# Second mixer: the forget term of the scores as a two-row product, the chunk mask as two more rows of queries and keys

## The reference, cut to what matters

```python
key_unit = jnp.arange(s) // causal_unit            # causal_unit: 64 in branch b, 1 in branch c
sc = jnp.einsum('bqhd,bkhd->bhqk', q_blk, k) * scale
if f_blk is not None:                              # branch c: F[t] - F[s]
    sc = sc + f_blk.transpose(0, 2, 1)[..., None] - f_k
mask = key_unit[None, :] <= q_unit[:, None]
sc = jnp.where(mask[None, None], sc, -jnp.inf)
p = jax.nn.softmax(sc, axis=-1)
...
log_f = jax.nn.log_sigmoid(c_f + b_forget)
f_cum = jnp.cumsum(log_f, axis=1)
out_c = block_causal_attention(heads(c_q), heads(c_k), heads(c_v), 1, f_cum)
```

## Time and profile before

| | |
|---|---|
| median of three runs | 2592.27 us (2592.19 to 2593.72) |
| profiled execution, its own time | 2591.27 us |
| its span, first to last instruction | 2589.5 us |
| TensorE busy | 2457.9 us, 95% of the span |
| VectorE busy | 1532.7 us, 59% |
| ScalarE busy | 1380.5 us, 53% |
| GpSimd busy | 185.5 us, 7% |
| mean granted clock of TensorE | 0.98 |

### The profile page before, as it was taken

How to read it: one execution, slowest core, us unless ns; L and a number is a source line. 1 busy time by engine, 2 the same in 40 slices (tenths; PEclk the granted TensorE clock), 3 DMA queues, 4 the chain that set the end, 5 groups by cost and what they waited for, 6 DMA issues and landing times.

```text
span 2589.5 us, 42657 instructions
## 1 busy us (share of the span) xinstructions
PE 2457.9 (95%) x17457; PEld 2289.9 (88%) x17457; DVE 1532.7 (59%) x1826; ACT 1380.5 (53%) x1828; POOL 185.5 (7%) x197
## 2 busy tenths in 40 slices
PE   7999999998999999999999999999889999997998
PEld 7998988998998998998999899898879988896997
DVE  5555667645555555567755555576575556747554
ACT  5555777255555545678535554545644444564443
POOL 0000113000000000012300000000030001003000
PEclk9999999999999999999999999999999999998999
DMA  6554443134554554443215456443345554334453
GB/s 220 185 180 146 147 131 115 66 122 150 178 184 162 178 183 159 147 144 126 90 54 175 148 192 206 146 129 109 120 130 183 190 182 141 120 113 148 154 184 125
DMA packets 312111, 385.89 MB, mean 149 GB/s; under 512 B 10780, under 2 KB 287280, under 8 KB 311984
## 3 DMA queue, kind: packets, MB, share of 16 engines
q1 hardware_dynamic: 311704, 384.00, 45.2%
q10 hardware_dynamic: 280, 0.10, 0.0%
HBM read 383.02 MB, written 1.06 MB: 148 GB/s over the span
## 4 chain that ended last, share of the span: by engine, by line
PE 75%; DVE 10%; ACT 9%; issue 4%; DMA 0%; POOL 0%; SPq 0%; DVEq 0%; ACTq 0%; POOLq 0%
PE bank L266 22%; PE bank L267 21%; PE bank L268 21%; DVE wlo L258 4%; ACT whi L252 4%; DVE arena L966 1%; PE bank L1237 1%; PE bank L1232 1%; PE bank L352 1%; PE bank L725 1%; DVE arena L2011 1%; ACT arena L1910 1%; ACT arena L318 1%; PE bank L1243 1%; PE bank L1209 1%
## 5 line engine op out<-in xcount | busy, mean ns | idle before, releaser
L258 DVE TENSOR_TENSOR wlo<-raw,whi 128x2048 fp32r<-128x2048 f32 x360 | 831.9, 2312 | 497.3 <-ACT whi L252 496.3
L266 PE MATMUL bank<-xhi,whi 128*128 128x256 f32 x3712 | 1065.5, 287 | 11.6 <-DVE arena L553 6.8
L267 PE MATMUL bank<-xlo,whi 128*128 128x256 f32 x3712 | 1053.5, 284 | 0.0
L268 PE MATMUL bank<-xhi,wlo 128*128 128x256 f32 x3712 | 1053.2, 284 | 0.0
L252 ACT ACTIVATE whi<-raw 128x2048 fp32r<-128x2048 f32 x360 | 681.7, 1903 | 104.7 <-PE bank L268 101.5
L266 PEld LDWEIGHTS bank<-xhi,whi 128*128 128x128 f32 x3712 | 715.0, 193 | 22.6 <-issue 16.8
L267 PEld LDWEIGHTS bank<-xlo,whi 128*128 128x128 f32 x3712 | 715.3, 193 | 4.9 <-issue 1.9
L268 PEld LDWEIGHTS bank<-xhi,wlo 128*128 128x128 f32 x3712 | 715.0, 193 | 0.0
L266 PE MATMUL bank<-whi,yhi 128*128 128x512 f32 x608 | 238.0, 391 | 9.2 <-ACT yhi L475 6.2
L267 PE MATMUL bank<-wlo,yhi 128*128 128x512 f32 x608 | 237.4, 390 | 0.0
L268 PE MATMUL bank<-whi,ylo 128*128 128x512 f32 x608 | 236.6, 389 | 0.0
(11 more groups left out here) (377 smaller groups left out, 2863.6 us busy)
## 6 DMA issues: line engine op xcount, KB each, us to landing
raw<-in_w_in SPq DMA_DIRECT2D x92, 1024.0 KB, 5.0
raw<-in_ffn_w_in SPq DMA_DIRECT2D x88, 1024.0 KB, 5.0
raw<-in_ffn_w_out SPq DMA_DIRECT2D x44, 1024.0 KB, 4.8
raw<-in_w_gate SPq DMA_DIRECT2D x32, 1024.0 KB, 5.4
raw<-in_w_up SPq DMA_DIRECT2D x32, 1024.0 KB, 5.5
raw<-in_w_down SPq DMA_DIRECT2D x32, 1024.0 KB, 4.8
raw<-in_w_branch_b SPq DMA_DIRECT2D x8, 1024.0 KB, 4.8
raw<-in_w_branch_a SPq DMA_DIRECT2D x8, 1024.0 KB, 4.8
```

The source lines that it names most:

```text
L258: e.tensor_tensor(wlo[s][:], raw[s][:], whi[s][:].bitcast(F32), ALU.subtract).then_inc(lo_done[s], 1)
L266: e.matmul(o, ahi, bhi, start=start, stop=False, skip_group_check=True)
L267: e.matmul(o, ahi, blo, start=False, stop=False, skip_group_check=True)
L268: return e.matmul(o, alo, bhi, start=False, stop=stop, skip_group_check=True)
```

## The change

Branch b: the queries get two more partitions (96 and 97) with the mask's value in one chunk of 64 and zero in the other, the keys two with ones and zeros, so that the score product over 98 partitions adds the chunk mask itself. VectorE writes these rows once per layer, at n = 8. Branch c: GpSimd spreads the log forget values, with sign plus and minus, into two columns of 32 for each head (`forget`); TensorE makes their running sums once, at n = 9, with three products into bank 4; VectorE takes them at n = 10 into `cum_q` and `cum_k`, whose two partitions 32h and 32h + 1 hold for head h the sum and ones, crosswise; and a head's forget term is one product over these two partitions in place of two (first 128 queries) and four (the rest). The tables `minus` and `chunk` leave the constants, two columns `even` and `odd` come in.

```diff
         def scores_b(e, h, o):
-            e.matmul(o[:, 0:128], bqh[0:96, h, 0:P], bkh[0:96, h, 0:P], start=True, stop=False, skip_group_check=True)
-            e.matmul(o[:, 0:128], mask_chunk, ident, start=False, stop=True, skip_group_check=True)
-            e.matmul(o[:, 128:384], bqh[0:96, h, P:T], bkh[0:96, h, :], start=True, stop=False, skip_group_check=True)
-            return e.matmul(o[:, 256:384], mask_chunk, ident, start=False, stop=True, skip_group_check=True)
+            e.matmul(o[:, 0:128], bqh[0:98, h, 0:P], bkh[0:98, h, 0:P], start=True, stop=True, skip_group_check=True)
+            return e.matmul(o[:, 128:384], bqh[0:98, h, P:T], bkh[0:98, h, :], start=True, stop=True, skip_group_check=True)
 
         def scores_c(e, h, o):
             p = slice(HD * (h % 2), HD * (h % 2) + HD)
             b = h // 2
-            G = CG[h % 2]
+            two = slice(32 * h, 32 * h + 2)
             k = dict(skip_group_check=True)
             e.matmul(o[:, 0:128], cq[p, b, 0:P], ck[p, b, 0:P], start=True, stop=False, **k)
-            e.matmul(o[:, 0:128], G[:, 0:128], ones2[:, 0:P], start=False, stop=False, **k)
-            e.matmul(o[:, 0:128], minus, G[:, 0:128], start=False, stop=False, **k)
+            e.matmul(o[:, 0:128], cum_q[two, 0:P], cum_k[two, 0:P], start=False, stop=False, **k)
             e.matmul(o[:, 0:128], mask_causal, ident, start=False, stop=True, **k)
             e.matmul(o[:, 128:384], cq[p, b, P:T], ck[p, b, :], start=True, stop=False, **k)
-            e.matmul(o[:, 128:384], G[:, 128:256], ones2, start=False, stop=False, **k)
-            e.matmul(o[:, 128:384], G[:, 256:384], ones2, start=False, stop=False, **k)
-            e.matmul(o[:, 128:384], minus, G[:, 0:256], start=False, stop=False, **k)
-            e.matmul(o[:, 256:384], minus, G[:, 256:384], start=False, stop=False, **k)
+            e.matmul(o[:, 128:384], cum_q[two, P:T], cum_k[two, :], start=False, stop=False, **k)
             return e.matmul(o[:, 256:384], mask_causal, ident, start=False, stop=True, **k)
+
+        def sums_pe(e, l):
+
+            e.wait_ge(*W["forget"](l))
+            e.wait_ge(*W["rope_done"](l, 1))
+            e.matmul(bank[4][:, 0:P], forget[:, 0, :], le, start=True, stop=True)
+            e.matmul(bank[4][:, P:T], forget[:, 0, :], ones, start=True, stop=False)
+            e.matmul(bank[4][:, P:T], forget[:, 1, :], le, start=False, stop=True).then_inc(W["sums"].sem, 1)
+
+        def mask_rows_dve(e, l):
+            for head, first, second in ((bqh, 0, MASKED), (bkh, 1, 1.0)):
+                rows = head[96:98, :, :].rearrange("p h (b i n) -> p h b i n", b=2, i=2)
+                e.memset(rows[:, :, :, 1 - first, :], 0.0)
+                for b, which in enumerate((even, odd)):
+                    up = e.tensor_scalar(rows[:, :, b, first, :], ones2[96:98, 0:64].unsqueeze(1).to_broadcast([2, H2, 64]),
+                                         which[96:98, :], second, ALU.mult, ALU.mult)
+            up.then_inc(W["mask_rows"].sem, 1)
+
+        def sums_dve(e, l):
+            e.wait_ge(*W["sums"](l))
+            e.tensor_scalar(cum_q, bank[4][:, 0:T], even, odd, ALU.mult, ALU.add)
+            e.tensor_scalar(cum_k, bank[4][:, 0:T], odd, even, ALU.mult, ALU.add).then_inc(W["sums_kept"].sem, 1)
@@ -1688,6 +1705,8 @@
                     values_pe(e, l, head2(n, 3))
+                if n == 9:
+                    sums_pe(e, l)
                 if n == MEAN_AT:
@@ -1756,9 +1775,10 @@
                 e.wait_ge(*W["rope_done"](l, 2))
+                e.wait_ge(*W["mask_rows"](l))
             else:
                 e.wait_ge(*W["kept"](l, 8))
-                e.wait_ge(*W["cg"](l, h))
+                e.wait_ge(*W["sums_kept"](l))
@@ -2019,6 +2039,10 @@
                     rope_dve(e, l)
+                if n == 8:
+                    mask_rows_dve(e, l)
+                if n == 10:
+                    sums_dve(e, l)
@@ -2096,19 +2120,20 @@
+            e.wait_ge(*W["lat_n"](l))
+            finish_waits(e)
+            e.memset(forget, 0.0).then_inc(W["forget_zero"].sem, 1)
             e.wait_ge(*W["lf"](l))
-            for h in range(H2):
-                if h >= 2:
-                    e.wait_ge(*W["scores"](l, 8 + h - 2))
-                finish_waits(e)
-                for a, (m, c) in enumerate(((le, 0), (ones, 0), (le, 1))):
-                    up = e.tensor_scalar(CG[h % 2][:, a * P:(a + 1) * P], m, lf[:, c * H2 + h:c * H2 + h + 1], None,
-                                         ALU.mult)
-                up.then_inc(W["cg"].sem, 1)
+            e.wait_ge(*W["forget_zero"](l))
+            finish_waits(e)
+            for i, sign in enumerate((1.0, -1.0)):
+                up = e.tensor_scalar(forget.rearrange("p c (h n) -> p c h n", n=32)[:, :, :, i],
+                                     lf.rearrange("p (c h) -> p c h", c=TT), sign, None, ALU.mult)
+            up.then_inc(W["forget"].sem, 1)
```

More of the change, by code:

```diff
@@ L93, in constants_2 @@
     freq[64:96, 0] = np.tile(inv_freq, 2)
-    parts = {"ones2": np.ones((P, T)), "minus": -np.ones((P, P)),
-             "chunk": np.where(r // 64 > c // 64, MASKED, 0.0), "causal": np.where(r > c, MASKED, 0.0),
-             "turn": turn, "freq": freq, "flip": r + c == P - 1}
+    parts = {"ones2": np.ones((P, T)), "causal": np.where(r > c, MASKED, 0.0),
+             "turn": turn, "freq": freq, "flip": r + c == P - 1,
+             "even": i[:, None] % 32 == 0, "odd": i[:, None] % 32 == 1}
     at, where = 0, {}
@@ L1517, in hybrid_stack_kernel @@
         rtmp = blk(17472)
-        CG = [blk(17984 + i * 384, 384) for i in range(2)]
+        forget = blk(17984, 256).rearrange("p (c n) -> p c n", c=TT)
+        cum_q, cum_k = blk(18240, 256), blk(18496, 256)
         table2 = blk(18944, CONSTANTS2.shape[1])
@@ L1532, in const2 @@
             return table2[:, a:b]
-        ones2, minus, mask_chunk, mask_causal, turn, freq, flip = [const2(n) for n in ("ones2", "minus", "chunk", "causal",
-                                                                                       "turn", "freq", "flip")]
+        ones2, mask_causal, turn, freq, flip, even, odd = [const2(n) for n in ("ones2", "causal", "turn", "freq", "flip",
+                                                                               "even", "odd")]
         cf_raw, cf_hi, cf_lo = [w[:, :, 0:H2] for w in ba_w]
@@ L1547, in hybrid_stack_kernel @@
             lf_shift=1, rowmax=12, bias_masked=1,
-            cg=4, scores=12, maxed=12, expd=12, inv=12, scaled=12, p_turned=12, pt_kept=12, o_product=12, o_hi=6, o_lo=6,
+            forget_zero=1, forget=1, sums=1, sums_kept=1, mask_rows=1, scores=12, maxed=12, expd=12, inv=12, scaled=12, p_turned=12, pt_kept=12, o_product=12, o_hi=6, o_lo=6,
             tap=31, mean=1, centred=1, c_sq=1, c_var=1, c_ln=1, c_r=1, c_norm=1, c_bias=1, c_abs=1, c_exp=1, c_l=1,
@@ L2098, in mix2_pool @@
             e.wait_ge(*W["bias_masked"](l))
+            e.wait_ge(*W["lat_n"](l))
+            finish_waits(e)
+            e.memset(forget, 0.0).then_inc(W["forget_zero"].sem, 1)
             e.wait_ge(*W["lf"](l))
-            for h in range(H2):
-                if h >= 2:
-                    e.wait_ge(*W["scores"](l, 8 + h - 2))
-                finish_waits(e)
-                for a, (m, c) in enumerate(((le, 0), (ones, 0), (le, 1))):
-                    up = e.tensor_scalar(CG[h % 2][:, a * P:(a + 1) * P], m, lf[:, c * H2 + h:c * H2 + h + 1], None,
-                                         ALU.mult)
-                up.then_inc(W["cg"].sem, 1)
[L2108 to L2111, removed]
+            e.wait_ge(*W["forget_zero"](l))
[4 more added lines that the diff above has]
+            up.then_inc(W["forget"].sem, 1)
+            e.wait_ge(*W["d_sig"](l))
+            finish_waits(e)
+            u = dpad[:, :, CONV_K - 1:]
+            e.tensor_tensor(u, u, rtmp2.rearrange("p (c t) -> p c t", c=2), ALU.mult).then_inc(W["u_done"].sem, 1)
             e.wait_ge(*W["c_sig"](l))
```

## The result

The changed kernel takes 2598.81 us (median of 17 runs, 2596.12 to 2602.94) against 2591.76 us before (17 runs, 2589.82 to 2595.4): ratio 1.0027, interval 1.0019 to 1.0034, so slower by 7 us. The profiled execution took 2596.32 us, 2.5 us under the median; its mean granted clock is 0.977, where the three slowest of the 17 (2600.93 to 2602.94 us) have 0.975 and the kernel before has 0.980, so its trace shows somewhat less lost clock than a slow execution has.

A forecast was written before the change was run, and what follows sets the result against it. TensorE was taken as the bound, joined to a VectorE-ScalarE ring. Per stage +2.24 + 0.66 - 0.44 - 4.40 = -1.94, twice -3.88, with one clock fall +1.68: -2.2, so 2590.1 us on the median; range 2585.0 to 2597.0.

The forecast's parts named there:

- Mask rows: Six VectorE instructions at n = 8 that nothing hides: 2.24 us per stage; TensorE then stands 2.63 us.
- the dearer of its two rows: For a memset of 512 elements, the two-input operation's step of about 0.60 us, taken over the copy's about 0.35.
- The clock: Granted clock falls to 0.50 behind TensorE's stall at n = 9, in one stage of two, costing 1.68 us.
- Branch c's head: Each head of branch c takes 2.74 us instead of 3.84, gaining 1.10 per head and 4.40 per stage.
- a dear return and a cheap fall: In branch c's heads, returning to 128 contracted rows costs 0.30 us, falling to fewer rows 0.10.
- Sums and branch b: Sums on TensorE at n = 9 add 0.66 us per stage; branch b's shorter scores gain 0.44.
- The ring: VectorE-ScalarE loop not limiting branch c; rival has it bind at n = 16 to 19: 2591.7 us, chance 0.12.
- The two-row rival: Changes of rows around branch c's two-row products eat all 1.10 us per head: +6.6 us, 2598.9, chance 0.10.

The follow-up runs named there:

- e1: Kernel before plus only the six mask-row instructions on VectorE at n = 8, unread: 2602.63 us, ratio 1.0036.
- e2: Kernel before with branch b's part alone, mask rows at n = 8, branch c as before: 2602.58 us, ratio 1.0038.
- e4: Whole change with the mask rows moved from n = 8 to n = 5: 2590.08 us, ratio 0.9994.
- e9: Kernel before with branch b's part alone, mask rows at n = 5: 2594.77 us, ratio 1.0010.
- e3: Kernel before with branch c's part alone, no mask rows, branch b keeping its mask products: 2587.19 us, ratio 0.9979.
- e6: e4 with a branch c head's products grouped 64, 64, 2, 2, 128, 128 rows; output lacks a part: 2587.79 us, ratio 0.9983.
- e11: Kernel before with branch c's part alone, products grouped by rows, sums at n = 13 and 14: 2582.39 us, ratio 0.9962.
- e8: e7 with the grouped product order of e6, including its missing output part: 2581.20 us, ratio 0.9954.
- e10: e8 with start=False in the second product, so that everything is computed: 2583.27 us, ratio 0.9968.
- e5: e4 with the forget product contracting 64 partitions in place of two, which changes the output: 2588.42 us, ratio 0.9987.
- e7: e4 with the sums moved to n = 13 on TensorE and n = 14 on VectorE: 2595.01 us, ratio 1.0008.

## Why the prediction was wrong

The forecast was 2590.1 us, -2.2; the median went up 7.0, past the range's end. In the profiled execution the spans differ by +5.1, 7.3 more than forecast, and the terms tell where:

- **Mask rows.** Right in kind and nearly in size: 2.36 us where 2.24 was forecast, and the stall 2.75 where 2.63 was. Twice 0.12 is 0.2 us. The tensor_scalars step 0.26 us as read; what is left of the 2.36, 1.32 us, are the two memsets, 0.66 each with the short idle time in front, where 0.60 was taken. The Trainium skill, VectorE: DVE Perf Modes, section Zero memsets can be issued as uint32 (trn2), gives a memset one cycle per element, and the prediction took from it that the dearer of its two rows holds; 0.66 agrees with that row's 0.60 and not with the 0.35 of the copy.
- **The clock.** This is the step that failed: "so I take a fall in one stage of the two: 1.68 us". The clock fell behind that stall in both stages, here and in e1 and e2, six times in six, and in e1, e2 and the first stage of after for 6.8 us and not 3.4. The prediction's own rows gave more than it took: eight falls behind ten stalls are 1.6 falls in two stages (an eleventh stall of 2.63 us, at the program's start, has a fall behind it too). That a fall would last longer they did not show; the clock was low for 3.4 us behind each of those eight. And I never asked what the wait at n = 15 would do, the one branch b's shorter scores would make longer. It grew from 0.88 to 1.34, and a fall stands behind it too, in both stages. Without falls the measured terms give 2 x (2.36 + 0.66 - 0.44 - 3.72) = -2.3; the stages grew by 3.2 + 2.0 = 5.2; so the falls cost 7.5 us where 1.7 was forecast, 5.8 of the 7.3. Pass by pass it is the same: n = 9 to 10 takes 3.42 and 2.26 us more than before in the two stages, of which the sums are 0.66, and n = 15 to 16 takes 0.57 and 0.58 more where a shorter head gives back 0.93; that is 2.8 + 1.6 + 1.5 + 1.5 = 7.4. e4 shows the first kind directly (-8.6 us with the rows moved, of which the work is 4.7), the second is seen in the granted clock and in the length of the pass at n = 15 (e4, e9). The two parts of the change alone add up to +4.4 us (e2, e3), the whole is +7.0; the 2.6 between are near the 3.0 of the two falls at n = 15, though the intervals are wider than that.
- **Branch c's head.** The mechanism was right, the size off: 0.93 us gained per head and not 1.10, 2 x 0.68 = 1.4 us of the 7.3. The term "So 1.74 + 2 x 0.30 + 4 x 0.10 = 2.74 us" was mis-sized, because I read the rows as a dear return and a cheap fall. The 0.30 of L1601 to L1603 was one whole change and half of the one before it, the 0.10 of L1603 to L1605 half a change: each costs 0.20 both ways (e6). The changed head has 1.30 us fewer columns and two changes more, 1.30 - 0.40 = 0.90. The rule that a change of mode drains TensorE (the Trainium skill, TensorEngine Tiling (Array Packing), Key Properties) fits the rows of these runs wherever the contracted rows go between 128, 64 and 2. From 128 to 96 or 98 nothing was seen: 0.22 a step in the earlier trace rows, and in the changed kernel the transposes lead into a head of 98 rows in 0.32 us and into one of 64 rows in 0.42.
- **Sums and branch b.** Right in size. (GpSimd's scalings that went were twelve a stage and not six, which changes nothing in the sum.) In the second stage, from n = 9 to n = 10 the lateness grew by 2.25, of which 0.66 are the sums and 1.6 the clock; from n = 11 to n = 15 it fell by 0.44, branch b's term.
- **The ring.** Right that it does not bind: at n = 19 ScalarE still waits for TensorE.

```profile
2290.24 0.84 ACT L1930 ACTIVATE arena<-bank,gate_bias 128x256 f32<-128x256 f32 x2 [0.76 <-PE bank L268]
```

It is 0.76 us where it was 1.68, by about the 0.93 that a head got shorter. With heads shorter still it does bind (e11). The two-row rival, which gave 2598.9 and so the measured time, hit it by luck and was wrong in its mechanism: e3 is 5.4 us faster.

**Open.** Behind waits of 1.33 and 1.34 us at n = 15 the clock fell in all 14 stages with branch c's new scores (after, e4 to e8, e10) and in one of four with the old ones (e2, e9). Behind waits of up to 0.88 at n = 15 (before, e1, e3, e11) it never did. What in the new scores favours the fall is not settled: not the two rows (e5) and not the number of changes of shape (e6). The whole shortened sequence remains, and was not taken apart further. The length of the wait alone does not decide either: in the kernel before TensorE waits 1.14 to 1.88 us at sixteen other places, and the clock is 1.00 over the 5 us behind each. Two falls of 6.8 us there, at 454.0 and 1266.4 us, have no wait over 0.1 us in the 10 us ahead of them, like the second falls of e7. Nor is it settled why a fall lasts 3.4 us in one place and 6.8 in another, and why e9's median is 3.5 us above what its work gives with no fall. Of the 4.4 us that e9's profiled span is over the earlier trace rows, the passes n = 9 to 20 hold 0.7, and 2.6 lie ahead of the first second-mixer stage, a part whose instructions no run changed and whose length differs from that of the kernel before by -1.6 (e2) to +4.2 us (e8). And the profiled executions leave 2 of the 7.0 us between the medians unread.

## What to carry to other kernels

Look for the place of small instructions before their length: the same six instructions cost 7 to 9 us where VectorE is full and TensorE waits behind it (e1, e4, e9), and lengthened no wait where VectorE has a gap. A stall in front of TensorE is to be priced with the clock behind it, at every place where the change lengthens a wait, also where it does so by making TensorE faster. Group f32 products by their number of contracted rows, and take a part of a change out if it only makes a waiting engine wait longer.

## What was new of the hardware

- The granted clock fell to 0.50 behind a wait of only 1.33 us (e4), in one stage of two behind the same wait and the same products (e9), and once in each stage with no wait in front of it (e7, at n = 17 and n = 16), while waits of 1.14 to 1.88 us elsewhere in the kernel before left it at 1.00.
- A fall lasted 3.4 us or 6.8 us; the one cost the path 1.5 to 1.6 us, the other 2.7 to 3.1.
- A change of the contracted rows between f32 products (128, 64, 2) costs 0.20 us in either direction, half of it on each side; six changes in a head against three made 2.91 us against 2.34.
- A VectorE memset of 512 f32 elements on two partitions is busy for 0.48 us and took 0.66 of the engine's time.
